# Recurrent (LRU) stage of a hybrid decoder step: two neighbour blocks of a gate product made one, and the second channel group laid between the output projection

## What is computed

```python
xc, new_buf = causal_conv(x_lru, conv_buf, conv_w, conv_b)
# rg_lru: 16 blocks of 80 channels, each with its own 80 x 80 gate maps
r = sigmoid(einsum('blnc,ncd->blnd', xb, w_a) + b_a)
i = sigmoid(einsum('blnc,ncd->blnd', xb, w_x) + b_x)
log_a = -LRU_C * r * softplus(-lam); a = exp(log_a)
u = sqrt(-expm1(2 * log_a)) * (i * xf)
h_t = a_t * h_(t-1) + u_t                       # scan over the tokens
lru_branch = (gelu(y_lru) * h) @ w_lru_out      # 1280 channels -> 1024
```

## Time and profile before

| | |
|---|---|
| runs | 2508.16, 2510.93, 2512.69 us; median 2510.93 us |
| the profiled execution | 2510.63 us; its span from first to last instruction is 2508.8 us |
| busy, share of the span | PE 97%, POOL 69%, DVE 47%, ACT 24% |
| granted clock of TensorE, mean | 0.989 of full speed |

### The profile page before, as it was taken

The page is one execution under the profiler, slowest core; times in us unless marked ns, Lnnn a source line. Parts: engine busy times, 40 slices in busy tenths (PEclk is TensorE's granted clock), DMA queues, the critical chain, the costliest instruction groups (busy, mean ns, idle before and its releaser), DMA issues.

```text
span 2508.8 us, 53186 instructions
## 1 busy us (share of the span) xinstructions
PE 2430.4 (97%) x19604; PEld 2374.5 (95%) x19604; DVE 1191.4 (47%) x1613; ACT 606.9 (24%) x869; POOL 1724.1 (69%) x1993
## 2 busy tenths in 40 slices
PE   7999999999989999999989999999999899999997
PEld 7899999999989999999988999999999899999997
DVE  6554555477463532022256554545874645221223
ACT  2313121325361211011113132222353612100111
POOL 5365757488787877777754757565887777777774
PEclk9999999999999999999999999999999999999998
DMA  4445545422223222322235546352222332223222
GB/s 162 166 154 173 173 169 180 144 91 89 87 82 90 93 92 85 94 97 85 92 126 195 179 148 208 137 192 107 91 91 84 79 94 92 92 88 97 92 83 85
DMA packets 120224, 298.61 MB, mean 119 GB/s; under 512 B 19136, under 2 KB 19648, under 8 KB 120064
## 3 DMA queue, kind: packets, MB, share of 16 engines
q1 hardware_dynamic: 60480, 199.78, 24.8%
q10 hardware_dynamic: 59584, 96.56, 11.3%
HBM read 255.92 MB, written 40.38 MB: 118 GB/s over the span
## 4 chain that ended last, share of the span: by engine, by line
PE 86%; DVE 5%; ACT 2%; DMA 2%; issue 2%; DVEq 2%; ACTq 1%; POOL 0%; POOLq 0%; SPq 0%
PE banks L369 79%; PE banks L535 2%; PE banks L497 1%; DVE scratch L878 1%; PE banks L551 1%; PE banks L527 1%; DMA scratch<-in_sret 1%; DVE scratch L1080 1%; PE banks L514 1%; DMA w_raw<-in_wstream 1%; DVE rinv L697 0%; ACT scratch L1306 0%; DVE scratch L980 0%; DVE scratch L1062 0%; PE banks L454 0%
## 5 line engine op out<-in xcount | busy, mean ns | idle before, releaser
L355 POOL TENSOR_TENSOR w_low<-w_raw,w_high 128x256 fp32r<-128x256 f32 (+1 forms) x1568 | 1287.3, 852 | 62.2 <-issue 0.8
L350 POOL TENSOR_SCALAR w_high<-w_raw 128x1024 fp32r<-128x1024 f32 (+3 forms) x420 | 437.6, 1042 | 699.1 <-PE banks L369 671.0
L369 PE MATMUL banks<-x_high,w_high 128*128 128x260 f32 x4096 | 835.8, 285 | 44.8 <-DVE scratch L1102 15.6
L369 PE MATMUL banks<-x_high,w_low 128*128 128x260 f32 x4096 | 828.5, 284 | 0.0
L369 PE MATMUL banks<-x_low,w_high 128*128 128x260 f32 x4096 | 826.8, 284 | 0.0
L369 PEld LDWEIGHTS banks<-x_high,w_high 128*128 128x128 f32 x4096 | 635.4, 190 | 55.6 <-issue 47.2
L369 PE MATMUL banks<-split_scratch,w_high 128*128 128x260 f32 x4000 | 643.5, 283 | 5.4 <-DVE split_scratch L1091 5.4
L369 PEld LDWEIGHTS banks<-x_high,w_low 128*128 128x128 f32 x4096 | 634.7, 189 | 0.0
L369 PEld LDWEIGHTS banks<-x_low,w_high 128*128 128x128 f32 x4096 | 634.2, 189 | 0.0
L369 PEld LDWEIGHTS banks<-split_scratch,w_high 128*128 128x128 f32 x4000 | 548.9, 189 | 6.4 <-issue 6.0
L369 PE MATMUL banks<-split_scratch,w_low 128*128 128x260 f32 x2000 | 403.2, 283 | 0.0
(11 more groups left out here) (157 smaller groups left out, 1773.7 us busy)
## 6 DMA issues: line engine op xcount, KB each, us to landing
w_raw<-in_wstream SPq DMA_DIRECT2D x268, 512.0 KB, 3.5
scratch<-in_sret ACTq DMA_DIRECT2D x64, 512.0 KB, 7.3
out_ret_s<-scratch ACTq DMA_DIRECT2D x64, 512.0 KB, 3.4
w_raw<-in_wstream SPq DMA_DIRECT2D x64, 384.0 KB, 3.0
w_raw<-in_wstream SPq DMA_DIRECT2D x40, 448.0 KB, 3.2
scratch<-v_rows ACTq DMA_DIRECT2D x64, 256.0 KB, 4.5
w_raw<-in_wstream SPq DMA_DIRECT2D x48, 320.0 KB, 2.8
out_ret_p<-scratch ACTq DMA_DIRECT2D x8, 512.0 KB, 2.8
```

The lines of the kernel that those rows point to most:

```text
L350: pool.tensor_scalar(WH[:, j, w], WR[:, j, w], 1.0, 0.0, ALU.mult, ALU.add)
L355: m = pool.tensor_tensor(WL[:, j, p], WR[:, j, p], WH[:, j, p].bitcast(F32), ALU.subtract)
L369: m = pe.matmul(out, wt[:, w, blk * P:(blk + 1) * P], x[xi], start=first and n == 0, stop=last and n == 2)
```

## The change

- `near` holds, for an inner tile, weights for its two neighbours at once. A block of 80 that crosses the tile's edge reaches at most 64 channels into the next tile, so the first 64 rows of tile t+1 and the last 64 rows of tile t-1 fit into one input tile of 128. r and i of inner tiles take 2 blocks each in place of 3, and `YG_UNIT` is 6 for every tile.
- That input tile is made by ACT: `neighbours(g,t)` copies two halves of 64 partitions of the high parts and two of the low parts into `XNH` and `XNL` (two buffers). PE waits for it (`xn_full`) where it waited for `xc_low`.
- `LRU_ORDER` puts `y(1,1)` ahead of the `out` tiles, `y(1,2)` in their middle, and `y(1,3)`, `y(1,4)` behind them. DVE's and ACT's work for group 1 is laid out anew to match. Two more tiles (`GLX`) take the outputs of channel tiles 5 and 6, and `gated_high(7)` waits until PE has done the last `out` tile.

```diff
@@ -46,14 +46,23 @@
 QK, GATES = 2 * KT, VT
-YG_UNIT = [(MT + 2 * len(BAND[t])) // 2 for t in range(GT)]
+PH = P // 2
+INNER = range(1, GT - 1)
+assert all(BAND[t] == [t - 1, t, t + 1] for t in INNER)
+assert all(((t + 1) * P - 1) // BLK * BLK + BLK <= (t + 1) * P + PH and t * P // BLK * BLK >= t * P - PH
+           for t in INNER)
+YG_UNIT = [(MT + 2 * 2) // 2] * GT
 X_EARLY = 4
 LRU_ORDER = ([("x", 0, t) for t in range(X_EARLY, GT)]
              + [w for t in range(GT) for w in (("y", 0, t), ("x", 1, t), ("ga", 0, t))]
-             + [("y", 1, 0), ("ga", 0, GT)] + [("out", 0, m) for m in range(MT)]
-             + [("y", 1, t) for t in range(1, GT)] + [("ga", 0, m) for m in range(GT + 1, MT)])
+             + [("y", 1, 0), ("ga", 0, GT), ("y", 1, 1)] + [("out", 0, m) for m in range(MT // 2)]
+             + [("y", 1, 2)] + [("out", 0, m) for m in range(MT // 2, MT)]
+             + [("y", 1, 3), ("y", 1, 4)] + [("ga", 0, m) for m in range(GT + 1, MT)])
+assert GT == 5 and MT - GT == 3
 LRU_UNITS = tuple(n for k, _, t in LRU_ORDER
                   for n in {"x": (MT,), "y": (YG_UNIT[t % GT],) * 2, "ga": (MT,), "out": (GT,)}[k])
@@ -139,6 +148,9 @@
 PC_GN, PC_CW, PC_CB, PC_BA, PC_BX, PC_BG, PC_SP = 0, 16, 56, 66, 76, 86, 102
 PCOLS = 112
+N_GLX = 2
 PIECE = 2
@@ -213,7 +226,14 @@
         STH, STL = R[:, o:o + ST_OFF[TT]], R[:, o + ST_OFF[TT]:o + 2 * ST_OFF[TT]]
         XCH, XCL = (rview(i * GT * TOK, GT, TOK) for i in range(2))
+        XNH, XNL = (rview((2 * GT + 2 * i) * TOK, 2, TOK) for i in range(2))
         GLH, GLL = (rview((2 * MT - 1 + i * GT) * TOK, GT, TOK) for i in range(2))
+        GL_HI = ([GLH[:, c, :] for c in range(GT)] + [GLX[:, c, :] for c in range(N_GLX)]
+                 + [GLH[:, c, :] for c in range(N_GLX, GT)])
+        GL_LO = ([GLL[:, c, :] for c in range(GT)] + [GLX[:, N_GLX + c, :] for c in range(N_GLX)]
+                 + [GLL[:, c, :] for c in range(N_GLX, GT)])
         MH, ML = rview(0, MT, TOK), rview(MT * TOK, MT, TOK)
         AH, AL = rview(0, FT, TOK), rview(FT * TOK, FT, TOK)
@@ -384,6 +404,10 @@
                 return [(hi[:, k, c * HALF:(c + 1) * HALF], lo[:, k, c * HALF:(c + 1) * HALF])
                         for c in range(2)]
+            def gated(c):
+                return [(GL_HI[c][:, n * HALF:(n + 1) * HALF], GL_LO[c][:, n * HALF:(n + 1) * HALF])
+                        for n in range(2)]
             def whole(ub, u, tb, idx, hi, lo, made=None, count=0):
                 tile_begin(tb, idx)
                 outs = [PP[:, slot(idx), c, 0:HALF] for c in range(2)]
@@ -597,16 +621,22 @@
                 def y_gates(g, t):
                     u, idx = B_Y[g][t], C_Y[g][t]
-                    q = spread(ub0, u, YG_UNIT[t], tb0, idx, XH, XL, range(MT), 0)
-                    pe.wait_ge(s["xc_low"], layer * LT + (g * GT + BAND[t][-1] + 1))
+                    q = spread(ub0, u, YG_UNIT[t], tb0, idx, [pairs(XH, XL, k) for k in range(MT)], 0)
+                    if t in INNER:
+                        n = g * len(INNER) + t - 1
+                        pe.wait_ge(s["xn_full"], layer * (GROUPS * len(INNER)) + (n + 1))
+                        xs = [pairs(XCH, XCL, t), pairs(XNH, XNL, n % 2)]
+                    else:
+                        pe.wait_ge(s["xc_low"], layer * LT + (g * GT + BAND[t][-1] + 1))
+                        xs = [pairs(XCH, XCL, k) for k in BAND[t]]
                     for w in range(2):
-                        q = spread(ub0, u, YG_UNIT[t], tb0, idx + 1 + w, XCH, XCL, BAND[t], q)
+                        q = spread(ub0, u, YG_UNIT[t], tb0, idx + 1 + w, xs, q)
                 def lru_out(ub, u, tb, idx):
                     tile_begin(tb, idx)
                     outs = [PP[:, slot(idx), c, 0:HALF] for c in range(2)]
                     for k in range(GT):
-                        m = product(outs, ub, u, k, pairs(GLH, GLL, k), k == 0, k == GT - 1)
+                        m = product(outs, ub, u, k, gated(k), k == 0, k == GT - 1)
                     m.then_inc(s["p_done"], 1)
                 def gate_a(m_):
@@ -620,11 +650,15 @@
                     gate_a(t)
                 y_gates(1, 0)
                 gate_a(GT)
+                y_gates(1, 1)
                 pe.wait_ge(s["gl_low"], layer * LT + GT)
-                for m_ in range(MT):
+                for m_ in range(MT // 2):
                     lru_out(ub0, B_OUT[m_], tb0, C_OUT[m_])
-                for t in range(1, GT):
-                    y_gates(1, t)
+                y_gates(1, 2)
+                for m_ in range(MT // 2, MT):
+                    lru_out(ub0, B_OUT[m_], tb0, C_OUT[m_])
+                y_gates(1, 3)
+                y_gates(1, 4)
                 for m_ in range(GT + 1, MT):
                     gate_a(m_)
@@ -632,9 +666,10 @@
                 with pe.Fori(0, MT // 2) as i:
                     for j in range(2):
                         place = (ub0 + 8 * i, B_MERGE + 2 * j, MERGE[0], tb0 + 4 * i)
-                        q = spread(*place, C_MERGE + 2 * j, XH, XL, range(MT), 0)
+                        q = spread(*place, C_MERGE + 2 * j, [pairs(XH, XL, k) for k in range(MT)], 0)
                         pe.wait_ge(s["gl_low"], layer * LT + LT)
-                        spread(*place, C_MERGE + 2 * j + 1, GLH, GLL, range(GT), q)
+                        spread(*place, C_MERGE + 2 * j + 1,
+                               [gated(c) for c in range(GT, LT)], q)
                 whole(ub0, B_WO, tb0, C_WO, MH, ML, s["mg_low"], layer * MT)
@@ -1088,7 +1123,7 @@
                 def gated_low(c):
                     dve.drain()
                     dve.wait_ge(s["gl_high"], layer * LT + (c + 1))
-                    tt(GLL[:, c % GT, :], YF[:, c % 2, :], GLH[:, c % GT, :].bitcast(F32), ALU.subtract
+                    tt(GL_LO[c], YF[:, c % 2, :], GL_HI[c].bitcast(F32), ALU.subtract
                        ).then_inc(s["gl_low"], 1)
                 def read_out(m_):
@@ -1122,30 +1157,53 @@
                         conv_low(1, t - 1)
                         gated_low(t - 1)
                     read_ga(t)
-                read_y(1, 0)
-                use_gates(1, 0)
                 scan(GT - 1)
                 conv_low(1, GT - 1)
                 gated_low(GT - 1)
+                read_y(1, 0)
+                use_gates(1, 0)
                 one_less_a2(GT)
                 use_ga(GT - 1)
                 read_ga(GT)
-                for m_ in range(MT):
-                    read_out(m_)
-                for t in range(1, GT):
-                    read_y(1, t)
-                    use_gates(1, t)
-                    scan(GT + t - 1)
-                    if t == 1:
-                        use_ga(GT)
-                    one_less_a2(GT + t)
-                    gated_low(GT + t - 1)
-                scan(LT - 1)
-                gated_low(LT - 1)
-                for m_ in range(GT + 1, MT):
-                    read_ga(m_)
-                for m_ in range(GT + 1, MT):
-                    use_ga(m_)
+                scan(GT)
+                gated_low(GT)
+                use_ga(GT)
+                read_y(1, 1)
+                use_gates(1, 1)
+                read_out(0)
+                one_less_a2(GT + 1)
+                read_out(1)
+                scan(GT + 1)
+                read_out(2)
+                gated_low(GT + 1)
+                read_out(3)
+                read_y(1, 2)
+                use_gates(1, 2)
+                read_out(4)
+                one_less_a2(GT + 2)
+                read_out(5)
+                scan(GT + 2)
+                read_out(6)
+                read_out(7)
+                gated_low(GT + 2)
+                read_y(1, 3)
+                use_gates(1, 3)
+                one_less_a2(GT + 3)
+                read_y(1, 4)
+                scan(GT + 3)
+                use_gates(1, 4)
+                one_less_a2(GT + 4)
+                read_ga(GT + 1)
+                gated_low(GT + 3)
+                scan(GT + 4)
+                gated_low(GT + 4)
+                read_ga(GT + 2)
+                use_ga(GT + 1)
+                use_ga(GT + 2)
                 dve.drain().then_inc(s["small_rd"], 1)
@@ -1451,7 +1509,10 @@
                 def gated_high(c):
                     act.wait_ge(s["gl_full"], layer * LT + (c + 1))
-                    A(GLH[:, c % GT, :], YF[:, c % 2, :], copy).then_inc(s["gl_high"], 1)
+                    if c == GT + N_GLX:
+                        act.wait_ge(s["p_done"], tb0 + (C_OUT[MT - 1] + 1))
+                    A(GL_HI[c], YF[:, c % 2, :], copy).then_inc(s["gl_high"], 1)
                 def gates(g, t):
                     c, idx = g * GT + t, C_Y[g][t]
@@ -1471,6 +1532,17 @@
                     act.wait_ge(s["t_free"], tb0 + (idx + 1))
                     A(YF[:, b, :], YF[:, b, :], ACT.Gelu_apprx_tanh).then_inc(s["y_gelu"], 1)
+                def neighbours(g, t):
+                    n = g * len(INNER) + t - 1
+                    g2, t2 = divmod(n - 2, len(INNER))
```

(65 more changed lines are left out.)

## The result

The changed kernel took 2486.95 us (median of 4 runs, 2483.57 to 2490.01) against 2511.08 us before. The ratio is 0.9905, with a 95% interval of 0.9888 to 0.9922: 24 us less, 0.95%. The profiled execution took 2490.0 us, with a span of 2488.2 us (2508.8 before); it is the longest of the four.

What follows compares the result with a forecast made beforehand. PE, busy 97% of the span, was taken as the bound. Removing 43.0 us, less 12.8 us of new stops (6.4 a layer), gave a net gain of 30.2 from 2510.6: 2480 us, range 2467 to 2494.

Steps and rivals of the forecast that it cites:

- What the change removes: LRU stage, both layers: 24 blocks 17.2 us, end stop 15.6, stop ahead of `out` 5.4, lost clock 4.8; sum 43.0 us.
- Step A: First tile: eight ACT copies ahead of `gates(0,0)` delay `use_gates(0,0)`, so PE stops 2.3 us at `y(0,1)`.
- The low bound of 0.35 us: Shortest time taken for a 64-partition ACT copy, if half the partitions were nearly half the work; PE's stop then 0.1 us.
- Step B: Group 1: DVE reaches `read_y(1,1)` late, so PE stops 2.3 us at `out(1)`; bounds 0.5 and 3.5.
- the walk: Queues of group 1 followed forward with the rows' durations, time 0 being the end of DVE's `read_ga(4)`.
- Step C: Weights beside the `out` tiles: POOL's low split falls behind PE, 1.0 us a layer, bounds 0 and 5.
- the upper bound of 5 us a layer: POOL's weight split beside the `out` tiles, with every split at some 1.2 us and DVE's and POOL's densest work overlapping.
- Step D: End of the stage: chains done 0.5 us before the merge's second tile; 0.3 us a layer taken, from 0 to 2.
- Step E: PE's clock lost behind four stops of 2.3 us: 0.5 us a layer, from 0 to 2.5.
- POOL becomes the bound: Rival, beside the `out` tiles: POOL's weight work costs 5 in place of 1 us a layer; 2488 us, chance 0.15.
- The stops only move: Rival: group 1's chains still end last and the merge waits as before; 2499 us, chance 0.07.

Runs made afterwards that it cites:

- conv_stores_late: Changed kernel with the three conv-row stores moved behind the merge loop, only the last-states store left ahead of it; 2475.79 us, ratio 0.9862 to the kernel before.
- stores_late: Changed kernel with ScalarE's four small stores (last states, conv rows) issued behind the merge loop, not ahead of it; 2476.47 us, ratio 0.9872 to the kernel before.

## Why the prediction was right

Predicted 2480, range 2467 to 2494; measured 2487. The direction, the size within a factor of 1.3 (24 for 30 us) and nearly every place were right. The largest part that was out, the stop in the merge with its clock, has one cause; two smaller errors fell the other way and helped.

- **What the change removes: right.** 43.0 us were counted, and the blocks, both stops and the clock behind them are gone. (The stops began at 656.6 and 740.4 us by the earlier trace rows, not at 656.3 and 740.1; nothing hangs on it.) Besides, two short stops of the old merge behind the low split (L355) went, 0.6 and 0.9 us, which I hadn't counted.
- **Step A: right, 2.3 predicted, 2.2 measured** (wait behind L1098). ScalarE, layer 0 (the first copy, the second, the last, the table load, the second sigmoid):

```profile
550.93 0.64 ACT L1508 ACTIVATE split_scratch<-scratch 128x520 fp32r<-128x520 f32 x1 [8.67 <-DVE scratch L1053]
551.47 0.62 ACT L1542 ACTIVATE split_scratch<-split_scratch 64x520 fp32r<-64x520 f32 x1
552.10 0.64 ACT L1543 ACTIVATE split_scratch<-split_scratch 64x520 fp32r<-64x520 f32 x1
...
556.01 0.63 ACT L1543 ACTIVATE split_scratch<-split_scratch 64x520 fp32r<-64x520 f32 x1
556.66 1.28 ACT L1521 ACT_TABLE_LOAD   x1
...
558.55 0.69 ACT L1524 ACTIVATE scratch<-banks,params_cur 128x520 f32<-128x520 f32 x1
```

A copy of 64 partitions takes 0.62 to 0.64 us, as that of 128, and the next one starts 0.63 to 0.66 us later. What the Trainium skill says in "ScalarE: Activation LUTs", section "What ACT_TABLE_LOAD costs" (time by elements per lane), is borne out by the length of these copies. The low bound of 0.35 us was far off.
- **Step B: place right, size 0.3 in place of 2.3 us.** VectorE, layer 0: `use_gates(0,0)` of step A, then `read_ga(4)`, `read_y(1,1)`, and the end of the stage:

```profile
559.27 0.70 DVE L1097 TENSOR_TENSOR scratch<-scratch 128x520 f32<-128x520 f32 x1 [6.53 <-ACT scratch L1524]
...
646.84 0.70 DVE L1137 TENSOR_TENSOR scratch<-banks,rinv 128x520 f32<-128x520 f32 x1 [0.16 <-PE banks L389]
...
668.41 0.70 DVE L1089 TENSOR_TENSOR scratch<-banks,rinv 128x520 f32<-128x520 f32 x1 [0.15 <-issue]
...
736.15 1.15 DVE L1126 TENSOR_TENSOR split_scratch<-scratch,split_scratch 128x520 fp32r<-128x520 f32 x1 [0.70 <-ACT split_scratch L1515]
737.46 0.70 DVE L1137 TENSOR_TENSOR scratch<-banks,rinv 128x520 f32<-128x520 f32 x1 [0.16 <-issue]
...
740.58 0.70 DVE L1215 TENSOR_TENSOR scratch<-banks,rinv 128x520 f32<-128x520 f32 x1 [0.47 <-issue]
742.58 0.70 DVE L1218 TENSOR_TENSOR scratch<-banks,scratch 128x520 f32 x1 [1.30 <-PE banks L389]
```

`read_ga(4)` ends at 647.54 and `read_y(1,1)` at 669.11, 21.6 us behind it; the walk had 22.6. PE for its part reached `out(1)` 1 us later, held up at `ga(5)`. Two errors of one microsecond in 22 make up the difference. Both fell on the lucky side for this term.
- **Step C: right in sum, wrong in place.** 1.0 us a layer predicted. Measured 0.9 at `ga(5)` and 0.3 at the last `out` tiles of each layer. I had looked among the `out` tiles. The weights' low split there took 951 ns for two blocks, between the 735 and 1033 of the earlier trace rows (POOL, 665 to 701 us; xcount | busy us, mean ns):

```profile
L375 POOL TENSOR_TENSOR w_low<-w_raw,w_high 128x256 fp32r<-128x256 f32 x20 | 18.6, 951 | 1.3
...
L370 POOL TENSOR_SCALAR w_high<-w_raw 128x640 fp32r<-128x640 f32 x7 | 5.1, 727 | 4.6 <-PE banks L389 3.1 <-DMA w_raw<-in_wstream 1.6
```

At `ga(5)` a unit of 8 blocks follows one of 6, which PE works through in 4.3 us, with DVE at work all the while: the high part and the first two low pieces end at 650.6, and PE goes on at 650.66 (POOL, layer 0):

```profile
646.09 1.50 POOL L370 TENSOR_SCALAR w_high<-w_raw 128x1024 fp32r<-128x1024 f32 x1
647.73 3.57 POOL L375 TENSOR_TENSOR w_low<-w_raw,w_high 128x256 fp32r<-128x256 f32 x3
```

The Trainium skill's "SBUF — State Buffer", section "🔬 SBUF: two separate sides", has an exclusive lock between the two engines. The trace agrees in kind, low pieces of one shape taking 0.73 or 1.2 to 1.6 us; its dearest reading, the upper bound of 5 us a layer, didn't come.
- **Step D: the chains right, the step itself wrong.** The walk had `gated_low(9)` at 89.6 and `read_ga(7)` at 90.4 on its scale. They ended at 89.8 and 90.6 (737.30 and 738.16 less 647.54), and DVE's next wait is on PE, so the chains did finish in time. What failed is the list of what the end of the stage lets loose. Behind `read_ga(7)`, `use_ga` and the drain stands `small_rd`, and behind that ScalarE's four stores. The prediction names neither them nor what they do to the load of weights: a term of nothing without a reason. Cost: 3.8 and 3.5 us of stop.
- **Step E: 0.5 us a layer predicted, 1.6 and 2.5 measured**, all of it behind the stop that wasn't foreseen. Behind the stops of 0.3 to 2.2 us the clock stayed at its full level in this run, though behind the same stop of step A a stretch of 3.4 us at half clock did begin at 559 us in conv_stores_late and at 1782 us in stores_late, each in one layer of two. That this term was small in the changed kernel is luck as well.

The sum with what was measured: 43.0 + 1.5, less A 4.4, B 0.6, C 2.5, the stores' stop 7.4 and the clock 4.1, gives 25.5 us. The two traces from which these terms come are 20.6 us apart in span; 23.6 of it lie in the stages of the change (the last column of the table above), and outside them the changed kernel's trace is 3 us longer. The medians are 24.1 us apart. So some 2 us of the sum aren't there; 0.8 of them are the merge's pairs, which take 9.37 us each in place of 9.31, for a reason that wasn't looked for. With B and the clock behind the stops of A and B as they were forecast (2.3 and 0.5 us a layer), the time would have come out some 5 us higher, at about 2492, still in the range. The rival "POOL becomes the bound" gave 2488 and so hit the time, but for a reason that the runs deny: of the 11.9 us of waits behind the low split, 7.4 stood behind a load that was late, 2.1 lie outside the LRU stage, and 2.5 are POOL's own. "The stops only move" is wrong too: the stops that were there are gone, and a third, hidden, came to light.

What is still open: the retention and feed-forward parts, which the change doesn't touch, differ from run to run by up to 4 us (from the last merge read of layer 0 to the first read of an x tile of layer 1 it was 909.8 to 913.6 us in these traces), so the last 1 to 3 us of any of these differences aren't explained.

## What to carry to other kernels

When a stall is taken away, list everything that is issued behind its end, the small stores too, and ask whose loads they meet now: a collision that lay under the old stall costs next to nothing until that day. Saving work on the busiest engine pays only in the stretches in which it is the bound; here the 12 blocks of group 1, 8.6 us, were worth nothing under the old order and 8 us under the new one. And a walk of the queues with durations from the trace came within a microsecond over 90 us, so it is worth its trouble wherever order is changed; what it can't show is an instruction that isn't on its list.

## What I had not expected of the hardware

- Three stores of 135 KB together, in pieces of 12 to 64 bytes, made a load of 448 KB on another queue take 9.2 us in place of 3.2, one of 384 KB 9.3 in place of 2.9 in the kernel before, and one of 512 KB 7.9 in place of 3.5 where stores_late has them. They took 8.3 to 10.7 us themselves to land in the kernel before, the one of 15 KB too; the store of 45 KB in pieces of 360 bytes ahead of them took 1.6.
- VectorE and GpSimd slow each other, both ways: the low split of two blocks took 735 ns beside a nearly idle VectorE and 951 to 1033 beside a busy one, and with the split on GpSimd lighter, the scan of 128 x 512 on VectorE took 1278 ns in place of 1570.
- A copy of 64 partitions on ScalarE costs as much as one of 128 (0.64 us): the prediction had taken this, but no row before had shown it.
